# Expert gates of two latent tiles scattered to memory by an adding indirect DMA, and two norm barriers removed

## The chip, the cores and the metric

One core of one Trainium2 chip runs the whole kernel. The metric is device microseconds (us) of that core for one execution, as the median of several runs.

## The reference, cut to what matters

Two trunk layers run over 640 tokens: 512 latent tokens and 128 context tokens, 1024 features, fp32. A layer is attention in four branches, gates, an output product, a second norm, and then a mixture of experts ("peer"), which is what the change is mostly about:

```python
q = (x @ wq).reshape(n, PEER_HEADS, 2, PEER_HALF)                   # 8 heads, two halves
s = jnp.einsum('nhpd,hpkd->nhpk', q, subkeys)                       # 128 sub-keys a half
sv, si = lax.top_k(s, PEER_TOPK)                                    # 16 of 128, twice
cand = sv[:, :, 0, :, None] + sv[:, :, 1, None, :]                  # 256 pairs
cv, ci = lax.top_k(cand, PEER_TOPK)                                 # 16 experts a head
experts = e1 * PEER_KEYS + e2                                       # of 16384
gates = jax.nn.softmax(cv, axis=-1)
u = jnp.take(u_tab, ec, axis=0); a = gelu(einsum('cd,ckd->ck', xc, u))
v = jnp.take(v_tab, ec, axis=0); out = einsum('ck,ckd->cd', gc * a, v)
```

Each token so picks 128 (expert, gate) pairs, 16 in each of 8 heads. Two heads of a token may pick the same expert; within one head all 16 differ.

## The kernel before, in words

The program is written by hand, engine by engine, with semaphores between them: the order in each engine's function is the order of execution. `phase_end` is a barrier of PE, ACT, DVE and POOL. SP issues the loads, ACT the stores.

**The expert stage.** For latent tokens nothing is gathered. All 16384 experts are computed in 128 chunks of 128 experts. A chunk's u block (512 KB) is loaded by SP, ACT casts its high part (`high_u`, L1029), DVE or POOL subtracts to get its low part (`low_u`, L1332 on DVE, L1505 on POOL), PE multiplies in three passes of 8 products (`u_chunk`, L763, 24 products of 128x512), ACT applies gelu (L1036) and stores the activations. Afterwards, in the v stage (L803), the activations are loaded again, multiplied on DVE by the gate of each (expert, token), L1458, and multiplied with the v blocks.

**The gates.** The v stage needs a table of gates by expert and token, which is nearly all zeros. For each tile of 128 tokens DVE first makes the choice (`choose`: maxima, indices, replacements, L1245 to L1405), PE turns it (L776), and then 32 batches of 4 tokens follow. In a batch DVE builds 8 one-hot tiles (L1433, L1434), PE multiplies them in 4 products (L785), ACT copies the result (L1090) and stores it later (L1046). PE does half a u chunk after each batch.

**The context tile** is treated by rows: its 128 u rows for each of 128 picks are gathered by POOL with an indirect DMA (`rows_of`, L1577) into a ring of four buffers, DVE takes the dot product of each (`dot`, L1413), POOL may fetch row set k once dot k-4 is done. DVE has one dot in each batch.

**Order of the stage.** The context tile is chosen first, then the latent tiles 0 to 3. PE does 12 chunks ahead (`AHEAD`), then for each latent tile 12 chunks beside the next choice and 16 chunks beside 32 batches (`BESIDE`), and 4 chunks at the end. The low parts of chunks that run beside a choice are made by POOL, those beside the batches by DVE. POOL also loads the next tile's sub-key scores (L1589) when a choice is done.

**The two norms.** After attention, barrier 2 ends, the heads of branch A are normed (ACT squares L987, PE sums L462, ACT root L990, DVE reciprocal and product L1304, L1306), barrier 3 follows, and the gate products (L473) begin. After the output product (`wout`, L462) comes barrier 4, then norm 2: ACT squares L826, PE sums, ACT root L828, DVE reciprocal L1145, barrier 5.

## Time and profile before

| | |
|---|---|
| median of 3 runs | 5435.64 us (5434.37 to 5435.89) |
| the profiled execution, its own time | 5430.56 us |
| its span in the trace | 5428.8 us |
| mean granted TensorE clock | 0.958 of full |
| PE busy | 5107.0 us, 94% of the span |
| DVE, ACT, POOL busy | 59%, 31%, 24% |

The page lists busy time by engine, the span in 40 slices, the DMA queues, and the chain of work that ended last: who released whom, backwards from the last instruction. "PEld" is PE's weight load, which overlaps its products. In a row `A <-B` means that an engine was idle and then released by B. Times of separate rows are of the profiled execution, counted from the start of its span. The second layer repeats the first 2648 us later.

### The profile page before, as it was taken

How to read it: one execution, taken by the hardware profiler on the slowest of the kernel's cores; microseconds unless marked ns; L12 is line 12 of the kernel's file. 1: busy time of each engine (PE TensorE's matmuls, PEld its weight loads, DVE VectorE, ACT ScalarE, POOL GpSimd, SP SyncE). 2: the span in 40 equal slices, each digit the busy share in tenths (PEclk: the TensorE clock that was granted, in tenths of full speed). 3: DMA queues.
4: the chain of work that ended last, by engine and by line, in shares of the span. 5: the costliest groups of instructions: out<-in, count | busy, mean ns of one | idle time of the engine just before them, and what ended most of it. 6: DMA issues, size and time to landing. Idle time of an engine off the chain costs nothing.

```text
span 5428.8 us, 68440 instructions
## 1 busy us (share of the span) xinstructions
PE 5107.0 (94%) x25520; PEld 4128.9 (76%) x25520; DVE 3206.4 (59%) x7233; ACT 1676.3 (31%) x2614; POOL 1322.4 (24%) x862
## 2 busy tenths in 40 slices
PE   4979899899999999999989798998899999999999
PEld 1846688677888887888867467977788888788887
DVE  1556411107998985666655753111488998766666
ACT  2324422222333332222232343212233333322222
POOL 1310022214344331111122001213244344211111
PEclk6978999999999999999999799999999999999999
DMA  6200022264877879888831000221367877888886
GB/s 227 71 30 1 11 72 69 71 256 161 273 247 258 277 255 313 291 292 288 288 104 54 15 1 30 72 65 63 129 215 261 280 261 241 314 287 291 292 288 222
DMA packets 349128, 981.98 MB, mean 181 GB/s; under 512 B 31648, under 2 KB 100128, under 8 KB 345504
## 3 DMA queue, kind: packets, MB, share of 16 engines
q1 hardware_dynamic: 215232, 553.19, 31.4%
q0 software_dynamic: 74880, 276.86, 14.5%
q10 hardware_dynamic: 58720, 148.04, 6.9%
q8 instruction: 179, 2.93, 0.2%
q14 instruction: 117, 0.96, 0.1%
HBM read 829.43 MB, written 148.54 MB: 180 GB/s over the span
## 4 chain that ended last, share of the span: by engine, by line
PE 85%; DVE 6%; DMA 3%; ACT 2%; POOL 1%; issue 1%; DVEq 1%; ACTq 0%; POOLq 0%; SPq 0%
PE PS L803 26%; PE PS L763 23%; PE PS L473 15%; PE PS L462 5%; PE PS L785 4%; PE PS L594 3%; PE PS L620 2%; PE PS L463 1%; DVE AR L1172 1%; PE PS L604 1%; POOL HR L1505 1%; DMA WR<-in_ada 1%; PE PS L564 1%; PE PS L751 1%; DVE SM L1211 1%
## 5 line engine op out<-in xcount | busy, mean ns | idle before, releaser
L803 PE MATMUL PS<-HB,VR 128*128 128x512 f32 x6144 | 1397.0, 390 | 17.2 <-DVE HB L1462 17.2
L803 PEld LDWEIGHTS PS<-HB,VR 128*128 128x128 f32 x6144 | 1156.2, 188 | 258.1 <-issue 18.1
L763 PE MATMUL PS<-HR,UR 128*128 128x512 f32 x4128 | 1013.3, 399 | 0.0
L1505 POOL TENSOR_TENSOR UR<-WR,UR 128x1024 fp32r<-128x1024 f32 x212 | 528.4, 2493 | 1784.2 <-ACT UR L981 933.9
L473 PE MATMUL PS<-HR,UR 128*128 128x320 f32 (+1 forms) x5952 | 924.5, 314 | 40.6 <-POOL HR L1505 40.0
L473 PEld LDWEIGHTS PS<-HR,UR 128*128 128x128 f32 x5952 | 887.6, 190 | 68.0 <-issue 45.4
L763 PEld LDWEIGHTS PS<-HR,UR 128*128 128x128 f32 x4128 | 768.2, 190 | 167.1
L1449 DVE TENSOR_TENSOR VR<-HT,VR 128x1024 fp32r<-128x1024 f32 x256 | 313.8, 1226 | 459.7 <-ACT VR L1102 398.0
L1102 ACT CAST VR<-HT 128x1024 fp32r<-128x1024 f32 x256 | 268.8, 1050 | 962.0 <-PE PS L803 959.5
L763 PE MATMUL PS<-HR 128*128 128x512 f32 x2016 | 486.8, 394 | 0.0
L763 PEld LDWEIGHTS PS<-HR 128*128 128x128 f32 x2016 | 372.2, 188 | 73.6
L1036 ACT ACTIVATE AR<-PS 128x512 f32<-128x512 f32 x256 | 153.3, 599 | 770.5 <-PE PS L763 753.9
L1434 DVE TENSOR_SCALAR AR<-CN,AR 128x128 f32<-128x128 f32 x1024 | 353.8, 346 | 0.0
L1433 DVE TENSOR_SCALAR AR<-CN,AR 128x128 f32<-128x128 f32 x1024 | 306.6, 300 | 28.6 <-issue 22.3
L1172 DVE RECIPROCAL AR<-AR 128x640 f32<-128x640 f32 (+2 forms) x40 | 172.5, 4312 | 190.0 <-ACT AR L882 189.8
L785 PEld LDWEIGHTS PS<-AR 128*128 128x128 f32 x2048 | 267.3, 191 | 22.6 <-DVE AR L1434 2.2
L1577 POOL DMA_INDIRECT HX<-in_vtab,AR x128 | 120.4, 940 | 627.7 <-DVE HX L1473 574.7
L785 PE MATMUL PS<-AR 128*128 128x128 f32 x2048 | 269.9, 275 | 0.0
L1090 ACT COPY AR<-PS 128x512 f32<-128x512 f32 x256 | 150.7, 589 | 325.1 <-PE PS L785 299.5
L1316 DVE TENSOR_TENSOR AR<-AR,PS 128x640 f32<-128x640 f32 x48 | 39.5, 823 | 348.1 <-PE PS L463 348.1
L1577 POOL DMA_INDIRECT AR<-in_urows,AR x128 | 163.2, 1275 | 269.7 <-DVE AR L1413 268.5
L594 PE MATMUL PS<-AR 32*128 32x512 f32 (+4 forms) x720 | 218.4, 486 | 10.8 <-ACT AR L896 10.8
(183 smaller groups left out, 5982.2 us busy)
## 6 DMA issues: line engine op xcount, KB each, us to landing
WR<-in_uT SPq DMA_DIRECT2D x256, 512.0 KB
HT<-in_vtab SPq DMA_DIRECT2D x256, 512.0 KB, 4.0
activations<-AR ACTq DMA_DIRECT2D x256, 256.0 KB
gates_by_expert<-AR ACTq DMA_DIRECT2D x128, 512.0 KB, 3.5
HW<-activations SPq DMA_DIRECT2D x256, 256.0 KB
WR<-gates_by_expert SPq DMA_DIRECT2D x64, 1024.0 KB
WR<-in_wgate SPq DMA_DIRECT2D x64, 640.0 KB, 3.9
WR<-in_ada SPq DMA_DIRECT2D x24, 1024.0 KB, 4.9
```

The lines of the kernel that those rows point to most:

```text
L462: pe.matmul(out(0, 512), lhsT, rhs(0, 512), start=start, stop=stop)
L473: last = pe.matmul(out(lo, hi), part(w, c), whole(h, c, lo, hi), start=start and i == 0, stop=stop and i == 2)
L594: last = pe.matmul(PF[:, at:at + hi - lo], q, k[:, lo:hi], start=True, stop=True)
L763: last = pe.matmul(bank(n % 2), u_part(n, w)[:, c, :], HR[:, h, c, 0:LAT], start=c == 0 and i == 0, stop=c == DC - 1 and i == 2)
L785: last = pe.matmul(bank(2 + m % 2)[:, P * k:P * k + P], HOT[:, m % 2, 2 * k, :], HOT[:, m % 2, 2 * k + 1, :], start=True, stop=True)
L803: last = pe.matmul(bank(d), VR[:, m % 4, w, P * d:P * d + P], HB[:, (m + 1) % 3, h, :], start=m == 0 and i == 0, stop=m == E1 - 1 and i == 2)
L1102: nc.scalar.copy(VR[:, m % 4, 0, :], VRAW[:, m % 4, :]).then_inc(vh_ready, 1)
L1433: nc.vector.tensor_scalar(HOT[:, m % 2, 2 * k, :], iota, EWT[:, 1, tok], None, ALU.is_equal)
L1434: last = nc.vector.tensor_scalar(HOT[:, m % 2, 2 * k + 1, :], iota, EWT[:, 0, tok], EWT[:, 2, tok], ALU.is_equal, ALU.mult)
L1449: nc.vector.tensor_tensor(VR[:, m % 4, 1, :], VRAW[:, m % 4, :], VR[:, m % 4, 0, :].bitcast(F32), ALU.subtract).then_inc(v_split, 1)
L1505: nc.gpsimd.tensor_tensor(dst, src, high.bitcast(F32), ALU.subtract).then_inc(sem_, 1)
L1577: pool.indirect_dma_start(dst, None, table, bass.IndirectOffsetOnAxis(ap=IDX.bitcast(U32)[:, k:k + 1], axis=0)).then_inc(sem_, 16)
```

## The change

**Scatter.** The gates of latent tiles 0 and 1 (`SCAT = 2`) no longer go through one-hot tiles. A table `gates_by_row` in memory (128 chunks x 128 experts x 256 tokens, 16.8 MB) is set to zero during attention by 8 stores of SP from a buffer that POOL clears. For these tiles DVE computes a row number for each pick, and POOL issues, for each of the 128 picks of a token tile, one indirect DMA that adds 128 single numbers (one for each token) into the table. After each head's 16 DMAs POOL waits until they have landed, since two heads may add to the same number. Tiles 2 and 3 keep the one-hot way, now with a whole chunk of PE in each batch instead of half a chunk. The v stage loads half of the gates from each table.

**Order.** The choices now come in the order tile 0, context, tile 1, tile 2, tile 3. PE does 36 chunks beside the first three choices, then for tiles 2 and 3 12 chunks and 32 chunks with 32 batches each, and 4 chunks. POOL makes no low parts in this stage: DVE makes all, twelve of them within and right behind each choice. SP loads the next tile's scores, not POOL. Each batch has two dots, not one. POOL's row fetches now stand between the scatters of tile 1, eight after each head.

**Norms.** The branch A norm has no barrier behind it: PE waits for it (`sub_done`) only ahead of the first product that reads the normed heads. Norm 2 has no barrier ahead of it: ACT squares each block of features as it is finished, and PE sums it in the loop of the output product, two blocks behind.

```diff
-AHEAD, BESIDE = 12, 16
+AHEAD, BESIDE = 12, 32
...
+SCAT = 2
+WIDE = SCAT * P
...
+                sp.wait_ge(zeroed, l + 1)
+                clear = gate_rows.rearrange("(n p t) a -> n p (t a)", p=P, t=4 * D)
+                for n in range(E1 * WIDE // (4 * D)):
+                    sp.dma_start(clear[n], UR[:, :, :, :].rearrange("p a b d -> p (a b d)").bitcast(F32)).then_inc(z_out, 16)
...
                 for n in range(E1):
                     load_u(n)
+                    if n - AHEAD - 3 in BEGIN[:-1]:
+                        i = BEGIN.index(n - AHEAD - 3)
+                        sp.wait_ge(picked, l * TILES + i + 1)
+                        sp.dma_start(S1, sub_rows[ORDER[i + 1]]).then_inc(ss_next, 16)
...
                 for j in range(2):
                     pe.wait_ge(sub_sq, l * 2 + (j + 1))
-                    both(cols(1024 * j), grp64, lambda lo, hi: HSQ[:, j, lo:hi], True, True).then_inc(sub_ss, 1)
-                phase_end(pe, l, 3)
+                    both(cols(2048 + 1024 * j), grp64, lambda lo, hi: HSQ[:, j, lo:hi], True, True).then_inc(sub_ss, 1)
...
                         last.then_inc(g_ready, 1)
+                        if k == 0:
+                            pe.wait_ge(sub_done, 2 * (l + 1))
...
-                phase_end(pe, l, 4)
-                norm(l, 1)
-                phase_end(pe, l, 5)
+                    if n >= 2:
+                        square_sums(l, n - 2)
+                for c in range(DC - 2, DC):
+                    square_sums(l, c)
+                phase_end(pe, l, 3)
...
-                for n in range(AHEAD):
+                for n in range(AHEAD * (SCAT + 1)):
                     u_chunk(n)
...
-                        u_chunk(n0 + AHEAD + m // 2, DC // 2 * (m % 2), DC // 2 * (m % 2 + 1))
+                        u_chunk(n0 + AHEAD + m)
...
+                    low_u(n0 + 2)
                     indices8(sub_keys, range(SUB // 2))
+                    low_u(n0 + 3)
                     indices8(sub_keys, range(SUB // 2, SUB))
...
-                        dot(g)
-                        if m % 2 == 0 and m >= 2:
-                            low_u(n0 + 13 + m // 2)
+                        if m >= 2:
+                            low_u(n0 + AHEAD + m)
+                        dot(2 * g)
+                        dot(2 * g + 1)
...
+                def scatter(t, h):
+
+                    for k in range(TOPK * h, TOPK * (h + 1)):
+                        pool.indirect_dma_start(gate_rows, bass.IndirectOffsetOnAxis(ap=SIDX.bitcast(U32)[:, t, k:k + 1], axis=0),
+                                                SW[:, t, k:k + 1], None, compute_op=ALU.add).then_inc(sc_out, 16)
+
+                def head_added(t, h):
+                    pool.wait_ge(sc_out, 16 * TOPK * (PH * (l * SCAT + t) + h + 1))
+
+                pool.wait_ge(z_out, 16 * (l + 1) * (E1 * WIDE // (4 * D)))
+                pool.wait_ge(picked, l * TILES + 1)
+                for h in range(PH):
+                    scatter(0, h)
+                    head_added(0, h)
+                pool.wait_ge(picked, l * TILES + 3)
+                for h in range(PH):
+                    scatter(1, h)
+                    for k in range(8 * h, 8 * h + 8):
+                        gather_u(k)
+                    head_added(1, h)
+                pool.nop().then_inc(scattered, 1)
+                for k in range(8 * PH, PICKS):
+                    gather_u(k)
```

POOL at the start of the expert stage, before (HR, UR: the low parts; S1 in HT: the scores; the rest: fetched rows of u):

```order
L1505 TENSOR_TENSOR UR<-WR,UR 128x1024 x2
L1589 DMA HT<-sub_key_scores 128x2048
L1577 DMA AR<-in_urows,AR 128x1024 x2
L1577 DMA HT<-in_urows,AR 128x1024
L1577 DMA WR<-in_urows,AR 128x1024
L1505 TENSOR_TENSOR HR<-WR,HR 128x8x128
```

And now, from the first instruction of the stage up to the second head of tile 1:

```order
L336 TENSOR_TENSOR IDLE<-CN 128x1
L1640 DMA gates_by_row<-AR 4194304x1 x144
L1629 DMA AR<-in_urows,AR 128x1024 x2
L1629 DMA HT<-in_urows,AR 128x1024
L1629 DMA WR<-in_urows,AR 128x1024
L1629 DMA AR<-in_urows,AR 128x1024 x2
L1629 DMA HT<-in_urows,AR 128x1024
L1629 DMA WR<-in_urows,AR 128x1024
L1640 DMA gates_by_row<-AR 4194304x1 x16
```

The first 144 scatters are the 128 of tile 0 and the first head of tile 1. The row fetches, which followed the context choice, now stand behind all of them and in eights between the heads.

DVE within the last third of a choice, before (L1383 to L1405 are the softmax's difference, the pair numbers and the weights):

```order
L1261 MAX_INDEX AR<-AR,HT 128x8 x8
L1383 TENSOR_TENSOR AR<-AR 128x128
L1392 TENSOR_TENSOR HT<-AR,CN 128x2048
L1395 TENSOR_TENSOR HT<-HT,AR 128x2048
L1397 TENSOR_REDUCE AR<-HT 128x128
L1401 TENSOR_REDUCE AR<-AR 128x8
```

And now, with the low parts of the u chunks (L1354) between:

```order
L1283 MAX_INDEX AR<-AR,HT 128x8 x8
L1354 TENSOR_TENSOR UR<-WR,UR 128x1024
L1413 TENSOR_TENSOR AR<-AR 128x128
L1422 TENSOR_TENSOR HT<-AR,CN 128x2048
L1425 TENSOR_TENSOR HT<-HT,AR 128x2048
L1427 TENSOR_REDUCE AR<-HT 128x128
L1354 TENSOR_TENSOR HR<-WR,HR 128x8x128
L1432 TENSOR_REDUCE AR<-AR 128x8
```

Ten low parts stand inside each choice and two right behind it; before, none did.

## Rows read from the trace of the kernel before

**Rows 1.** The page: the chain that ended last, share of the span by line.
```profile
PE PS L803 26%; PE PS L763 23%; PE PS L473 15%; PE PS L462 5%; PE PS L785 4%; PE PS L594 3%; PE PS L620 2%; PE PS L463 1%; DVE AR L1172 1%; PE PS L604 1%; POOL HR L1505 1%; DMA WR<-in_ada 1%; PE PS L564 1%; PE PS L751 1%; DVE SM L1211 1%
```
**Rows 2.** Chain pieces of layer 0's expert stage: start us, us, what.
```profile
1232.66 58.16 PE PS L763 x240
1484.90 63.65 PE PS L763 x276
```
**Rows 3.** Chain around the last batches of that stage.
```profile
2032.46 0.89 PE PS L785 x8
2033.35 2.79 PE PS L763 x12
```
**Rows 4.** PE's timeline: the last u products of layer 0.
```profile
2055.58 6.44 PE L763 MATMUL PS<-HR,UR 128*128 128x512 f32 x27
```
**Rows 5.** DVE's timeline: one choice of a latent tile, cut.
```profile
1483.08 0.29 DVE L1245 MAX8 AR<-HT 128x8 f32<-128x128 f32 x1
...
1524.02 4.34 DVE L1395 TENSOR_TENSOR HT<-HT,AR 128x2048 f32<-128x2048 f32 x1
...
1533.16 2.29 DVE L1395 TENSOR_TENSOR HT<-HT,AR 128x2048 f32<-128x2048 f32 x1
1535.53 2.29 DVE L1397 TENSOR_REDUCE AR<-HT 128x128 f32<-128x2048 f32 x1
```
**Rows 6.** DVE's timeline in a batch: dot, low part, then one-hots until the next dot.
```profile
1560.12 1.21 DVE L1413 SCALAR_TENSOR_TENSOR HT<-HT,PS 128x1024 f32<-128x1024 f32 x1
...
1561.26 1.22 DVE L1332 TENSOR_TENSOR UR<-WR,UR 128x1024 fp32r<-128x1024 f32 x1
1562.40 0.28 DVE L1433 TENSOR_SCALAR AR<-CN,AR 128x128 f32<-128x128 f32 x1
...
1564.21 1.22 DVE L1413 SCALAR_TENSOR_TENSOR WR<-WR,PS 128x1024 f32<-128x1024 f32 x1
```
**Rows 7.** Timeline of POOL and DVE: scores load, four row fetches in a row, next choice.
```profile
1300.38 0.75 POOL L1589 DMA_DIRECT2D HT<-sub_key_scores  x1
1301.43 1.01 POOL L1577 DMA_INDIRECT AR<-in_urows,AR  x1 [0.30 <-issue]
...
1305.24 0.94 POOL L1577 DMA_INDIRECT WR<-in_urows,AR  x1 [0.30 <-issue]
...
1307.05 0.29 DVE L1245 MAX8 AR<-HT 128x8 f32<-128x128 f32 x1 [11.30 <-issue]
```
**Rows 8.** POOL's timeline: a row fetch issued beside the one-hot tiles of a batch.
```profile
1575.71 1.68 POOL L1577 DMA_INDIRECT HT<-in_urows,AR  x1 [1.77 <-DVE HT L1413]
```
**Rows 9.** DMA issues: count, KB each, median us to landing.
```profile
out_st_kr<-AR ACTq DMA_DIRECT2D x2, 16.0 KB, 3.2
...
WR<-in_vtab,AR POOLq DMA_INDIRECT x64, 4.9
```
**Rows 10.** Timeline of layer 0's branch A norm, with the products ahead and behind.
```profile
640.48 0.57 PE L463 MATMUL PS<-AR,CN 128*128 128x128 f32 x2
...
649.09 0.88 DVE L1306 SCALAR_TENSOR_TENSOR HT<-HT,SM,AR 128x640 f32<-128x640 f32 x1
...
650.51 9.09 PE L473 MATMUL PS<-HR,UR 128*128 128x320 f32 x48
```
**Rows 11.** Timeline around norm 2 of layer 0: last residual, first and last sum, barrier.
```profile
1018.30 1.01 DVE L1322 SCALAR_TENSOR_TENSOR XT<-PS,MD,XT 128x512 f32<-128x512 f32 x2 [7.64 <-PE PS L463]
...
1020.27 1.12 PE L462 MATMUL PS<-AR,CN 128*128 128x512 f32 x2 [0.48 <-ACT AR L826]
...
1028.80 0.38 PE L463 MATMUL PS<-AR,CN 128*128 128x128 f32 x2
...
1034.40 0.06 DVE L332 MEMSET IDLE<- 128x1 f32 x1 [0.20 <-DVEq L342]
```
**Rows 12.** Busy time by stretch: attention and v stage of layer 0 (clock, DMA share, GB/s last).
```profile
369.00:638.00 269.00, 243.14 (x1315) 166.25 (x1314) 157.53 (x468) 132.47 (x349) 5.03 (x4) 0.90 0.02 6
2075.00:2760.00 685.00, 685.00 (x3023) 567.38 (x3022) 455.50 (x503) 195.14 (x249) 115.67 (x123) 1.00 0.84 283
```

More of the change, by code:

```diff
@@ L96 @@
 C_EPS = C_I16 + 16
-C_ALL = C_EPS + 1
+C_ROW = C_EPS + 1
+C_ALL = C_ROW + 1
 TRIG = 6 * LAT
@@ L234, in build @@
         n_ = Arena(AR, 0, AF)
+        n_.take(12 * TOK)
         NSQ, NSTD, NRS = n_.take(DC, TOK), n_.take(TOK), n_.take(TOK)
@@ L319, in build @@
         a_in, g_in = [sem(f"activations_in{k}") for k in range(4)], [sem(f"gates_in{k}") for k in range(2)]
+        zeroed, z_out, sc_out, scattered = sem("zeros_made"), sem("gate_rows_cleared"), sem("gate_rows_out"), sem("gate_rows_done")
+        gs_in = [sem(f"gate_rows_in{k}") for k in range(2)]
         hw_ready, hbh_ready, h_ready, v_used = (sem(n) for n in ("expert_gated", "expert_gated_high", "expert_gated_split", "v_used"))
@@ L499, in norm, with square_sums @@
                 last.then_inc(ss_ready, 1)
+            def square_sums(l, c):
+                pe.wait_ge(sq_ready, l * (2 * DC) + (DC + c + 1))
+                last = both(cols(2048), ones, lambda lo, hi: NSQ[:, c, lo:hi], c == 0, c == DC - 1)
+                if c == DC - 1:
+                    last.then_inc(ss_ready, 1)
             def project(l, n):
@@ L766, in u_chunk @@
                         last.then_inc(u_used, 1)
-                for n in range(AHEAD):
+                for n in range(AHEAD * (SCAT + 1)):
                     u_chunk(n)
-                for t in range(LTILES):
-                    n0 = AHEAD + PER_TILE * t
+                for t in range(SPREAD):
+                    n0 = BEGIN[SCAT + 1 + t]
                     for n in range(n0, n0 + AHEAD - 1):
                         u_chunk(n)
-                    pe.wait_ge(picked, l * TILES + t + 2)
+                    pe.wait_ge(picked, l * TILES + SCAT + t + 2)
                     for i in range(3):
@@ L1003, in _ @@
                     sigmoid(l, DC - 1, k)
-                for n in range(2):
-                    high(l, B_WQ + n)
-                phase_end(act, l, 4)
                 norm(l, 1)
-                phase_end(act, l, 5)
+                high(l, B_WQ + 1)
+                phase_end(act, l, 3)
                 high_h(l, 1)
@@ L1414, in dot, with expert_number @@
                                                    accum_out=DOT[:, k:k + 1]).then_inc(dotted, 1)
-                choose(0, EWC)
-                nc.vector.scalar_tensor_tensor(EWC[:, 0, :], EWC[:, 0, :], float(PK), EWC[:, 1, :], ALU.mult, ALU.add)
-                dve.drain()
-                nc.vector.tensor_scalar(IDX.bitcast(U32), EWC[:, 0, :], GN[:, G_FIRST:G_FIRST + 1], None, ALU.add)
-                dve.drain().then_inc(picked, 1)
-                for t in range(LTILES):
-                    n0 = AHEAD + PER_TILE * t
-                    choose(t + 1, EW)
+                def expert_number():
+                    nc.vector.scalar_tensor_tensor(EW[:, 0, :], EW[:, 0, :], float(PK), EW[:, 1, :], ALU.mult, ALU.add)
+                    dve.drain()
+                for i in range(SCAT + 1):
+                    choose(i, BEGIN[i])
+                    expert_number()
+                    if ORDER[i] == LTILES:
+                        nc.vector.tensor_copy(WC, EW[:, 2, :])
+                        nc.vector.tensor_scalar(IDX.bitcast(U32), EW[:, 0, :], GN[:, G_FIRST:G_FIRST + 1], None, ALU.add)
+                    else:
+                        t = ORDER[i]
+                        nc.vector.tensor_copy(SW[:, t, :], EW[:, 2, :])
+                        nc.vector.tensor_scalar(EW[:, 1, :], EW[:, 0, :], float(WIDE), CN[:, C_ROW:C_ROW + 1], ALU.mult, ALU.add)
+                        dve.drain()
+                        nc.vector.tensor_scalar(SIDX[:, t, :].bitcast(U32), EW[:, 1, :], float(P * t), None, ALU.add)
+                    dve.drain().then_inc(picked, 1)
+                    low_u(BEGIN[i] + AHEAD)
+                    low_u(BEGIN[i] + AHEAD + 1)
+                for t in range(SPREAD):
+                    n0 = BEGIN[SCAT + 1 + t]
+                    choose(SCAT + 1 + t, n0)
                     dve.nop().then_inc(picked, 1)
-                    dve.wait_ge(ewt_ready, l * LTILES + t + 1)
+                    low_u(n0 + 12)
+                    dve.wait_ge(ewt_ready, l * SPREAD + t + 1)
                     settled(dve)
+                    low_u(n0 + 13)
                     for m in range(BATCHES):
```

175 lines of the change are left out of this document (90 added, 85 removed).

## The prediction

> **What bounds the kernel now.** I read the chain of waits first [rows 1]: almost all of it is PE, the v stage (L803, 26%), the u products (L763, 23%) and the gate products (L473, 15%). The one-hot products that the change halves (L785) are 4% of it. So PE sets the end, and one-hot work is worth what it takes on PE, not what it takes on DVE. The edits lie in the expert stage before the v stage, which begins in layer 0 at 1232.66 [rows 2] and whose last product ends at 2055.58 + 6.44 = 2062.0 [rows 4]: 829.4 us. Next I read PE's unit prices from the chain: 276 u products take 63.65 us [rows 2], so a chunk of 24 takes 5.54; half a chunk takes 2.79 and the 4 one-hot products of a batch 0.89 [rows 3]. 128 chunks and 128 batches make 709 + 114 = 823 us of 829: the stage is PE from end to end. DVE in a batch takes 1.81 us for the 8 one-hot tiles (1562.40 to 1564.21), 1.14 for a dot and 1.14 for a low part every second batch [rows 6], 3.5 us against PE's 3.68: nearly full, but not the bound.
>
> **One-hot batches removed.** 64 of 128 a layer at 0.89 us of PE: **-57 us a layer**. A remaining batch now has a whole chunk, PE 5.54 + 0.89 = 6.43 us; DVE needs 1.81 + 1.14 + two dots 2.28 = 5.2 us. DVE does not bound it.
>
> **Low parts moved to DVE.** Twelve stand in and behind each choice. A choice's own work runs from 1483.08 to 1535.53 + 2.29 = 1537.8, 54.7 us; one product in it took 4.34 us where its twin took 2.29 [rows 5], beside POOL's subtraction, which goes: 52.7. Ten low parts inside add 11.4 and the tail (sum, weights, row numbers, some eight small instructions) an estimated 2.3: 66.4 us to "picked". Then the next scores must be loaded. Before, that took from 1300.38 to 1307.05 [rows 7], 6.7 us; SP now does it without POOL in between, and the two low parts behind the choice lie beside it. Period 73.1 us against PE's 12 x 5.54 = 66.4. Three periods and the fourth choice end at 3 x 73.1 + 66 = 285 us, where PE alone would be at chunk 47 at 260 plus 3 us of its slow start (240 products in 58.16 us [rows 2]): **+22 us a layer**. The fifth choice has its scores early, and DVE enters it some 12 us ahead of PE: nothing.
>
> **POOL: the scatters.** No row shows an adding scatter. The nearest row is the row fetch, also an indirect DMA of 128 entries: 0.94 us busy, and 1.25 us from start to start when nothing blocks it (1301.43 to 1305.24, three intervals with their 0.30 of issue) [rows 7]. I take s = 1.25 us. Bounds: below, 0.75, the busy time of a direct DMA on POOL [rows 7]; above, 1.68 + 0.30 = 1.98, the fetch that falls beside DVE's one-hots [rows 8]. Small transfers land 3.2 us after issue [rows 9].
> Tile 0's scatters begin at 66 us (first choice) and take 8 x (16 x 1.25 + 3.2) = 186: until 252. Tile 1 was picked at 213 and starts then; its first head goes out until 272, and its first four fetches until 277, in time for the first batch at 290. But POOL's fetches number 4 to 7 wait for dots 0 to 3, so its second head starts only at 297. From here each of the 7 heads costs 16 x 1.25 = 20 us in which no row is fetched, and then a chain: the first row lands 4.9 us after issue [rows 9], two dots 2.3, the next batch's one-hots and low part 3.0, two dots 2.3, the eighth fetch 1.25, together 13.8. That is 33.8 us for four batches, where PE needs 4 x 6.43 = 25.7. DVE stands in a dot, its next one-hots stand behind it, and PE waits for them. 297 + 7 x 33.8 = 534, the last batches' dots and chunk 79 bring PE to 549; PE alone from 285 needs 5.5 + 0.7 + 32 x 6.43 = 212, so 497: **+52 us a layer**. Some two issues a head fall beside one-hots and take 0.74 longer [rows 8], 8 x 1.5 = **+12**. In the second one-hot tile POOL has only two fetches a batch, 2.5 to 4 us of 6.43: nothing.
> PE's idle pieces are some 8 us each. If it restarts at a lower clock, POOL still sets the period: I add nothing.
>
> A rule bears on the +12. The Trainium skill (GPSIMD Engine Reference, Key points) says that GpSimd shares its SBUF interfaces with VectorE, with contention against instructions in a two-port mode "or with two SBUF inputs". The traces agree for the one-hots (1.68 against 0.94 us). By its second half the low parts and dots would hold issues too, and if a third of the 256 scatters paid 0.74 the layer would have 63 us more, not 12; the fetches of the v stage that run beside two-input products at 0.94 us speak against it.
>
> **Zeroing.** 16.8 MB; at the 283 GB/s of the v stage it takes 59 us, in an attention stage of 269 us whose DMA share is 0.02 [rows 12]. POOL has 5 us of work there. Nothing; uncovered it would be 59 us a layer.
>
> **v stage.** The gate product becomes two of half size; DVE is busy 455 of 685 us there and PE all of it [rows 12]. The same bytes are loaded. Nothing.
>
> **Branch A norm.** Before, PE's sums end at 641.1 and the gate products start at 650.51 [rows 10]. Now 48 of them, about 9 us, run while DVE norms; the first product that reads the normed heads waits until 650.0. From there all is as before, minus these 9: **-9 us a layer**.
>
> **Norm 2.** Last residual 1018.30, barrier passed 1034.40 [rows 11]. The squares are hidden now, but PE's sums are not: the output product is PE-bound (DVE waits 7.64 us a block), so the 6 sums in its loop push its end by 6 x 1.1 = 6.7 us (8 took from 1020.27 to 1029.18). Then come the last residual 1.0, its square and sum, some 1.8, and the 5.2 from last sum to barrier (1029.18 to 1034.40), with a cast and the root's table load of ACT now between: 14.7 and 1 to 2 against 16.1. **0**, between -1.5 and +1.
>
> **Sum.** -57 + 22 + 52 + 12 - 9 = +20 us a layer, +40 in two: 5430.56 + 40 = 5470.6 for the profiled execution. The median of the runs stands 5.1 above that execution: **5476 us**, +0.7%. About 0.2% (11 us) is what a measurement of this kernel can tell from no change.
>
> **Rivals.**
> 1. *The scatters hide, and PE stays the bound: faster.* The point is s: POOL's period 16 s + 13.8 falls to PE's 25.7 at s = 0.75. Then the layer has -57 + 22 - 9 = -44: 5348 us. At s = 0.94 (busy time alone, the 0.30 of issue not paid) 16 s + 13.8 is 28.8 and the layer stands at about -25: 5386. The two signs meet near s = 1.1, only 0.15 below the row's spacing. For it: a scatter moves 512 bytes where a fetch moves 512 KB, and the fetches may land sooner than 4.9 us. Against it: POOL's issue time is of 128 entries, not of bytes.
> 2. *The adding scatter is dearer than a fetch: much slower.* To add, the old number must be read too, three accesses an entry where a fetch has two. Half again of 0.94 and 0.30 of issue makes s = 1.71. Tile 0 then ends at 66 + 8 x 30.6 = 311, the first head of tile 1 and its fetches at 352, seven periods of 41.2 bring 640, PE is at chunk 80 at 655: POOL costs 158, the layer +114 (no separate port term is large beside it, 0 to 12 left in), 5664 us. At the upper bound 1.98 the same steps give 724, the layer +183: 5802. The Trainium skill (Collectives: The Full Stack, Why ReduceScatter is half of AllGather) says that an add needs two source reads, two read descriptors per chunk on one ring; by it the fetch is too low a price for the scatter. No row here shows that.
> 3. *The parts cancel*: s near 1.1, within 11 us of before.
> That the batches would not go, or a barrier not, is excluded by the order of instructions.
>
> **Chances.** The forecast (s 1.15 to 1.4: 5445 to 5520) 0.34; rival 2 with all above 1.4, 0.25; rival 1, 0.32; rival 3, 0.09. So slower 0.59, faster 0.32, same 0.09. Signs are mixed, so the range runs from s = 0.75 to s = 1.98: 5345 to 5810.
>
> **What would show it.** Right: POOL's scatters start 1.25 us apart; tile 0's last lands near 250 us of the stage; in the first one-hot tile PE stops once for each head for about 8 us, released by one-hots (DVE) that stood behind a dot that waited for a row fetch; that tile takes some 265 us from its first batch to chunk 80, the next 206; the gate products start 9 us earlier after attention; norm 2 as before. Wrong if POOL is idle between heads, if PE is whole in that tile, if the spacing is far from 1.25, or if low parts make PE wait in the batches too. A stage of about 790 us would be rival 1, one over 900 rival 2.

## The result, and the profile after

The changed kernel takes 6219.8 us (median of 4 runs), the kernel before 5435.0: 1.144 times as long, 95% interval 1.142 to 1.146. The forecast was 5476 us, slower by 0.7%, with a range to 5810: the sign was right, the size was not, and the time lies outside the range. The profiled execution took 6220.68 us with a span of 6218.8 (before 5430.56 and 5428.8), at a mean granted clock of 0.894 in place of 0.958. Among the runs of the experiments three executions, two of the kernel before and one of tile0_only, were in a slower state; the ratios leave them out, and without it tile0_only's median of 5665.3 would be 5660.8.

The page of the changed kernel: the clock in 40 slices, the software DMA queue, the chain that ended last by line (rows 1 before), and two groups of instructions (busy, mean ns of one, idle time ahead of them and what ended it).

```profile
PEclk6979999999577799999999799999965768999999
...
q0 software_dynamic: 147456, 268.76, 16.1%
...
PE PS L823 22%; POOL gates_by_row L1640 13%; PE PS L484 13%; PE PS L783 8%; PE PS L473 5%; PE PS L611 3%; PE PS L637 2%; DMA AR<-in_urows,AR 1%; DVE AR L1194 1%; PE PS L621 1%; PE PS L474 1%; PE PS L805 1%; POOL HR L1558 1%; DMA gates_by_row<-AR 1%; DMA WR<-in_ada 1%
...
L1640 POOL DMA_INDIRECT gates_by_row<-AR x512 | 856.5, 1673 | 741.6 <-issue 564.1
...
L805 PE MATMUL PS<-AR 128*128 128x128 f32 x1024 | 151.0, 295 | 833.3 <-DVE AR L1482 833.3
```

Before, the chain had no scatters and POOL was 1% of it. Now the scatters (L1640) are 13% and the u products (L783) have shrunk from 23% to 8%. PE waited 833 us in two layers ahead of its one-hot products (L805). An issue is busy 1.67 us on the mean, and POOL was idle for 564 us ahead of scatters although nothing that the profile knows was to be waited for ("issue"). The two low stretches of the clock, 5 to 7 tenths, are those waits of PE.

A measure that serves below is the **stage**: layer 0's expert stage, from the matmul behind the barrier (L338) to the first v product. It is 838.6 us before (1232.08 to 2070.7) and 1240.8 now (1233.71 to 2474.5). That is 402 us a layer more, all of the difference of 790 and a little over. A **quiet** head is one that is scattered while DVE makes no choice. The first and the second **one-hot tile** are the token tiles 2 and 3, which keep the one-hot way, with the u chunks beside them.

POOL's timeline in the changed kernel, where tile 0's scatters begin: start us, us, and in brackets the idle time ahead of each and what ended it.

```profile
1303.78 2.04 POOL L1640 DMA_INDIRECT gates_by_row<-AR  x1 [69.85 <-DVEq L1464]
1306.12 1.57 POOL L1640 DMA_INDIRECT gates_by_row<-AR  x1 [0.30 <-issue]
1308.00 1.56 POOL L1640 DMA_INDIRECT gates_by_row<-AR  x1 [0.30 <-issue]
1312.86 1.58 POOL L1640 DMA_INDIRECT gates_by_row<-AR  x1 [3.30 <-issue]
1314.74 1.57 POOL L1640 DMA_INDIRECT gates_by_row<-AR  x1 [0.30 <-issue]
1316.62 1.56 POOL L1640 DMA_INDIRECT gates_by_row<-AR  x1 [0.30 <-issue]
1320.28 1.56 POOL L1640 DMA_INDIRECT gates_by_row<-AR  x1 [2.10 <-issue]
```

Two things are to be seen. An adding scatter of 128 entries keeps POOL busy for 1.56 us where a fetch of 128 rows took 0.94 [rows 7]. And the first three go out some 2 us apart, then POOL stands for 3.3 us; from there on one to three go out between pauses of 1.8 to 5.7 us. The eight heads of tile 0 run from 1303.78 to 1681.3, 47 us a head where 23 had been forecast; the last three, with no choice beside them, take 41.

Busy time by stretch in layer 0 (columns: length, then PE, PEld, DVE, ACT and POOL, each with its number of instructions, then granted clock, DMA share, GB/s):

```profile
1530.00:1727.00 197.00, 2.73 (x12) 1.89 (x10) 0.28 (x1) 1.53 (x2) 118.53 (x78) 0.52 0.19 5
1727.00:2148.00 421.00, 199.52 (x905) 165.84 (x905) 153.58 (x377) 57.44 (x84) 241.81 (x171) 0.73 0.51 136
2148.00:2447.00 299.00, 295.39 (x1408) 245.51 (x1407) 250.38 (x670) 92.30 (x132) 64.41 (x68) 0.99 0.82 277
```

For 197 us PE does nothing: it has done the first batch of the first one-hot tile and wants the one-hots of the second batch, DVE stands in the first dot ahead of them, the row for that dot has not been fetched, and the fetch stands in POOL's queue behind tile 0's scatters and the first head of tile 1. In the next 421 us PE is busy less than half the time: seven more times it stops for 29.4 to 32.5 us, 30.9 on the mean. Then, with all scatters gone, it is full. POOL's timeline shows the period of a head, from the first fetch behind one head's scatters to the first fetch behind the next, and PE's shows one of the stops:

```profile
1722.25 1.00 POOL L1629 DMA_INDIRECT AR<-in_urows,AR  x1 [0.31 <-issue]
...
1736.18 2.67 POOL L1640 DMA_INDIRECT gates_by_row<-AR  x1 [0.30 <-issue]
...
1780.39 1.00 POOL L1629 DMA_INDIRECT AR<-in_urows,AR  x1 [0.30 <-issue]
```

```profile
1790.29 2.08 PE L805 MATMUL PS<-AR 128*128 128x128 f32 x8 [29.36 <-DVE AR L1482]
```

Eight fetches with the dots that they wait for take 13.9 us (1722.25 to 1736.18), then 16 scatters 44.2: 58 us, and 59.1 on the mean of seven, where PE needs 25.7.

### The profile page after: what moved, and what is told of

The parts are those of the page before. It is cut to its first block, busy times and chain, and to the rows that moved or that the text cites. A ratio compares the mean times of both kernels' runs of the same rounds, so it can differ in the third digit from the quotient of the medians.

```text
span 6218.8 us, 65850 instructions
## 1 busy us (share of the span) xinstructions
PE 5046.3 (81%) x24476; PEld 4051.8 (65%) x24476; DVE 3098.5 (50%) x6595; ACT 1603.1 (26%) x2478; POOL 1776.6 (29%) x1244
## 3 DMA queue, kind: packets, MB, share of 16 engines
q0 software_dynamic: 147456, 268.76, 16.1%
## 4 chain that ended last, share of the span: by engine, by line
PE 59%; POOL 15%; issue 10%; DVE 7%; DMA 4%; ACT 2%; DVEq 1%; ACTq 0%; POOLq 0%; SPq 0%
PE PS L823 22%; POOL gates_by_row L1640 13%; PE PS L484 13%; PE PS L783 8%; PE PS L473 5%; PE PS L611 3%; PE PS L637 2%; DMA AR<-in_urows,AR 1%; DVE AR L1194 1%; PE PS L621 1%; PE PS L474 1%; PE PS L805 1%; POOL HR L1558 1%; DMA gates_by_row<-AR 1%; DMA WR<-in_ada 1%
## 5 line engine op out<-in xcount | busy, mean ns | idle before, releaser
L1640 POOL DMA_INDIRECT gates_by_row<-AR x512 | 856.5, 1673 | 741.6 <-issue 564.1
L783 PE MATMUL PS<-HR,UR 128*128 128x512 f32 x4128 | 1017.3, 404 | 14.3 <-DVE UR L1354 14.3
L484 PEld LDWEIGHTS PS<-HR,UR 128*128 128x128 f32 x5952 | 887.1, 190 | 65.5 <-issue 45.5
L783 PEld LDWEIGHTS PS<-HR,UR 128*128 128x128 f32 x4128 | 790.8, 194 | 198.2 <-DVE UR L1354 18.6
L805 PE MATMUL PS<-AR 128*128 128x128 f32 x1024 | 151.0, 295 | 833.3 <-DVE AR L1482 833.3
L1558 POOL TENSOR_TENSOR UR<-WR,UR 128x1024 fp32r<-128x1024 f32 x132 | 314.8, 2386 | 1590.2 <-ACT UR L1005 945.5
L805 PEld LDWEIGHTS PS<-AR 128*128 128x128 f32 x1024 | 145.6, 208 | 849.7 <-DVE AR L1482 840.2
L1444 DVE SCALAR_TENSOR_TENSOR AR<-AR,PS 128x1024 f32<-128x1024 f32 x128 | 152.0, 1214 | 940.8 <-DMA AR<-in_urows,AR 940.8
L783 PE MATMUL PS<-HR 128*128 128x512 f32 x2016 | 493.0, 401 | 12.0 <-DVE HR L1354 12.0
L783 PEld LDWEIGHTS PS<-HR 128*128 128x128 f32 x2016 | 386.8, 194 | 95.5 <-DVE HR L1354 14.2
L1113 ACT COPY AR<-PS 128x512 f32<-128x512 f32 x128 | 75.2, 588 | 844.1 <-PE PS L805 842.0
L1354 DVE TENSOR_TENSOR UR<-WR,UR 128x1024 fp32r<-128x1024 f32 x172 | 209.1, 1220 | 166.4 <-ACT UR L1051 161.9
L1629 POOL DMA_INDIRECT AR<-in_urows,AR x128 | 121.9, 952 | 331.4 <-DVE AR L1444 319.5
```

What stands on the lines that cost most here:

```text
L484: last = pe.matmul(out(lo, hi), part(w, c), whole(h, c, lo, hi), start=start and i == 0, stop=stop and i == 2)
L783: last = pe.matmul(bank(n % 2), u_part(n, w)[:, c, :], HR[:, h, c, 0:LAT], start=c == 0 and i == 0, stop=c == DC - 1 and i == 2)
L805: last = pe.matmul(bank(2 + m % 2)[:, P * k:P * k + P], HOT[:, m % 2, 2 * k, :], HOT[:, m % 2, 2 * k + 1, :], start=True, stop=True)
L1558: nc.gpsimd.tensor_tensor(dst, src, high.bitcast(F32), ALU.subtract).then_inc(sem_, 1)
L1629: pool.indirect_dma_start(dst, None, table, bass.IndirectOffsetOnAxis(ap=IDX.bitcast(U32)[:, k:k + 1], axis=0)).then_inc(sem_, 16)
L1640: pool.indirect_dma_start(gate_rows, bass.IndirectOffsetOnAxis(ap=SIDX.bitcast(U32)[:, t, k:k + 1], axis=0), SW[:, t, k:k + 1], None, comp ...
```

## The experiments

Twelve kernels. Stages are of layer 0; each time is a median, each ratio against runs of the kernel before on the same chip.

| run | time, us | ratio (95%) | stage, us |
|---|---|---|---|
| no_scatter | 5339.9 | 0.9825 (0.9811 to 0.9839) | 802.5 |
| norms_only | 5409.7 | 0.9962 (0.9949 to 0.9975) | 837.8 |
| one_tile2k | 5411.1 | 0.9957 (0.9941 to 0.9973) | 842.2 |
| one_tile | 5461.9 | 1.0049 (1.0031 to 1.0068) | 864.0 |
| spread2k_plain | 5468.3 | 1.0055 (1.0034 to 1.0076) | 870.8 |
| spread2k | 5477.3 | 1.0078 (1.0063 to 1.0093) | 866.5 |
| plain2k | 5586.7 | 1.0282 (1.0261 to 1.0303) | 928.7 |
| plain_scatter | 5647.1 | 1.0394 (1.0379 to 1.0409) | 943.0 |
| tile0_only | 5665.3 | 1.0416 (1.0394 to 1.0437) | 963.4 |
| spread | 5703.9 | 1.0491 (1.0468 to 1.0513) | 983.4 |
| space2k | 5929.2 | 1.0915 (1.0899 to 1.0931) | 1100.3 |
| moved_only | 6213.9 | 1.1428 (1.1405 to 1.1452) | 1243.7 |

**No scatters at all.** This asks whether the other terms of the forecast hold.

```diff
-                for h in range(PH):
-                    scatter(0, h)
-                    head_added(0, h)
...
-                    scatter(1, h)
...
-                    head_added(1, h)
```

> The changed kernel without any scatter and without the waits for them (the gates of two latent tiles stay zero, so their expert sums are left out); zeroing, loads, choices and the low parts on DVE stay. If the scatters are the whole loss, the prediction's other terms are left: 64 batches fewer -57, low parts on DVE +22, norm -9 us a layer, stage near 829 - 57 + 22 = 794 us and 5430.6 - 88 = 5343 us for the profiled execution, PE whole in both one-hot tiles but for the start of the first. If DVE with all low parts is itself a bound (the rival), the first one-hot tile still shows PE waiting for one-hots in every batch, the stage is 830 us or more and the time no less than 5420 us.

Measured: 5339.9 us; the stage is 802.5 in layer 0 and 804.2 in layer 1, against 838.6 and 838.2 before. So everything in the change but the scatters gains 1.75%, and the scatters cost 438 us a layer. PE and its clock by stretch, then the start of the first one-hot tile:

```profile
1522.00:1728.00 206.00, 206.00 (x1025) 172.99 (x1024) 168.85 (x423) 65.32 (x96) 59.34 (x64) 1.00 0.91 307
...
1796.00:2002.00 206.00, 206.00 (x1022) 172.99 (x1021) 168.63 (x415) 64.57 (x95) 58.32 (x62) 1.00 0.89 297
```

```profile
1522.39 1.05 PE L805 MATMUL PS<-AR 128*128 128x128 f32 x8
1523.19 5.82 PE L783 MATMUL PS<-HR,UR 128*128 128x512 f32 x24
1528.86 1.05 PE L805 MATMUL PS<-AR 128*128 128x128 f32 x8
```

Both one-hot tiles take the 206 us of 32 x 6.43 with PE busy throughout, and a batch comes every 6.47 us. The rival that DVE with all low parts would bound the batches is out. The first batch is at 290.6 us of the stage; the forecast had 290.

**Tile 0's scatters alone.**

```diff
                 for h in range(PH):
-                    scatter(1, h)
                     for k in range(8 * h, 8 * h + 8):
                         gather_u(k)
-                    head_added(1, h)
```

> The changed kernel with tile 0's scatters alone (tile 1's are left out, its gates stay zero). It parts the 438 us a layer that the scatters cost: tile 0's heads end at 446 us of the stage, and the first fetches stand behind them, where PE wants the first at 290. If that start is one of two causes, the stage is 802 + 446 + 5 - 290 = 963 us, 5340 + 2 x 161 = 5662 us, and the other 277 us a layer are tile 1's heads between the fetches. If tile 1's heads alone were the loss (tile 0's hidden, as the prediction had it), 5345 us.

Measured: 5665.3 us, stage 963.4, both as expected. PE's waits have one entry of one-hots, twice (once a layer):

```profile
PE PS L805 <- DVE AR L1482: 318.6, 2, 159.7
```

So of the 438 us, 161 are the late first fetch, and 277 are tile 1's heads: one head of 41 before the first fetch, and seven periods of 59.1 (the seven from 1722.25 to 2135.96) against PE's 25.7, which is 41 + 7 x 33.4 = 275.

**More memory for descriptors, and its control.**

```diff
-                   dynamic_dma_scratch_size=1024)
+                   dynamic_dma_scratch_size=2048)
...
-        PT = t_.take(2, 640)
+        PT = QA
...
-        WC, IDX, DOT = p_.take(PICKS), p_.take(PICKS), p_.take(PICKS)
+        WC = GN[:, G_LAM:G_LAM + PICKS]
+        IDX, DOT = p_.take(PICKS), p_.take(PICKS)
```

> The changed kernel with twice the memory for the descriptors of POOL's indirect DMAs (2048 bytes a partition in place of 1024); two small buffers move for it (the turned probabilities into QA, the context weights into GN). Theory A (space): in the changed kernel the scatters go out 1.87 us apart in twos and threes and then pause 2 to 5 us, since three adding scatters fill the memory and the next waits until one has been worked off. Then here some seven go out in a row before the first pause, and if the DMA engines keep up the spacing is 1.87 us throughout: a head of tile 0 takes 16 x 1.87 + 3.0 = 33 us in place of 41, the expert stage near 990 us in place of 1212, 5780 us in all. Theory B (work-off rate): the 16 DMA engines work off one adding scatter in about 2.6 us whatever the memory; then the first six or seven go out in a row, but the head still takes some 40 us and the time stays within 1% of 6220 us. Theory C (the pauses have nothing to do with memory, they are in POOL's own routine): pattern and time as in the changed kernel.

> The control for the run with 2048 bytes: the changed kernel with the two small buffers moved, the descriptor memory left at 1024 bytes. If the memory is what let seven scatters go in a row in place of three, this one shows threes again and 6220 us within 0.3%. If the moved buffers did it, some 5930 us.

Measured: 5929.2 us with 2048 bytes; 6213.9 with the buffers moved alone (the line with 1024 kept), the same as the changed kernel. POOL's timeline with 2048 bytes, first, seventh and eighth scatter:

```profile
1295.07 2.05 POOL L1641 DMA_INDIRECT gates_by_row<-AR  x1 [69.89 <-DVEq L1465]
...
1306.76 1.56 POOL L1641 DMA_INDIRECT gates_by_row<-AR  x1 [0.30 <-issue]
1310.21 1.56 POOL L1641 DMA_INDIRECT gates_by_row<-AR  x1 [1.90 <-issue]
```

Seven go out in a row in place of three. In the control the fourth again waits 3.23 us. So it is the memory, theory A; C is out. The quiet heads of tile 0 take 34.7 us (two of them from 1532.49 to 1601.89) in place of 41, close to 16 x 1.86 + 3 = 33, so B, a limit of the DMA engines' rate near 2.6 us a scatter, is out for them as well. My 5780 us were too low all the same: beside the choices a head still takes 37 to 43, and in tile 1's part a period is some 50 us in place of 59, the pauses being shorter but not gone ("issue" idle time ahead of scatters 291 us of two layers, after 564; both hold the 0.30 of each issue, at most 154).

**Scatters that overwrite, with either memory.**

```diff
-                                                SW[:, t, k:k + 1], None, compute_op=ALU.add).then_inc(sc_out, 16)
+                                                SW[:, t, k:k + 1], None).then_inc(sc_out, 16)
```

> The changed kernel with scatters that overwrite in place of adding (a token that picks one expert in two heads keeps only the last weight, so that part of the result is left out). Theory A (the add makes it dear, by the read of the old number, a third access for each entry): busy time of an issue falls from 1.56 to about the fetch's 0.94 us, three accesses become two, so that five or more fit before a pause; spacing 1.25 to 1.6 us, stage 830 to 900 us in place of 1212, 5430 to 5600 us in all. Theory B (4-byte writes to memory are dear in themselves): busy time falls, the pauses grow by as much, a head of tile 0 still takes 36 to 41 us and the time stays above 6000 us.

> Scatters that overwrite (as in plain_scatter, so part of the result is left out) with 2048 bytes for descriptors. With 1024 seven of them went out in a row before a pause; if a plain scatter takes half the room of an adding one and the room is all there is, fourteen go here, about one pause in a head of 16 is left, and a head of tile 0 takes 16 x 1.26 + 3 = 23 us beside quiet engines in place of 25 to 26: stage some 20 us shorter than plain_scatter's, 5590 to 5620 us against 5647. If the DMA engines' rate makes the pauses, they come back behind the first fourteen and the time stays above 5630 us.

Measured: 5647.1 and 5586.7 us. POOL's timeline with 1024 bytes: the first, seventh and eighth scatter,

```profile
1299.73 1.47 POOL L1640 DMA_INDIRECT gates_by_row<-AR  x1 [69.85 <-DVEq L1464]
...
1307.83 0.96 POOL L1640 DMA_INDIRECT gates_by_row<-AR  x1 [0.30 <-issue]
1310.78 0.96 POOL L1640 DMA_INDIRECT gates_by_row<-AR  x1 [1.99 <-issue]
```

and with 2048 bytes the first, the fourteenth and the fifteenth:

```profile
1293.00 1.48 POOL L1641 DMA_INDIRECT gates_by_row<-AR  x1 [69.95 <-DVEq L1465]
...
1310.96 0.96 POOL L1641 DMA_INDIRECT gates_by_row<-AR  x1 [0.30 <-issue]
1314.88 0.97 POOL L1641 DMA_INDIRECT gates_by_row<-AR  x1 [2.96 <-issue]
```

Before the first pause, three and seven go out with the add, seven and fourteen without: an adding scatter takes about twice the room of a plain one, and the room grows with the memory. Without the add an issue is busy 0.96 us, the fetch's price. The add is thus the larger part of the damage: 1240.8 - 943.0 = 298 of the 438 us. The pauses were not all that expectation A made of it: the plain scatters with 1024 bytes still cost 141 us a layer, above the 830 to 900 us of stage that I had written down, since "seven in a row" still means one or two pauses in a head, and a plain scatter beside the choices takes up to 3.03 us. With 2048 bytes the fourteen came as expected; the stage is 14 us shorter and not 20, and 5586.7 us lies 3 us below what was written down. The rule that the forecast cited as rival 2's (the Trainium skill, Collectives: The Full Stack, Why ReduceScatter is half of AllGather: an add has two source reads and so two read descriptors) agrees with both halves, the price of an issue and the room that it takes; the runs show the effects, not the descriptors.

**The same work in another order.** Six heads of tile 0 first, then two scatters behind each pair of fetches in place of 16 in a row:

```diff
+                done = scatters(0, 96)
+                pool.wait_ge(picked, l * TILES + 2)
+                for k in range(PICKS):
+                    if k == 2 * BATCHES + 4:
+                        done = scatters(done, 36)
+                    gather_u(k)
+                    if k >= 5 and k % 2:
+                        done = scatters(done, 2)
+                done = scatters(done, SCAT * PICKS)
```

> The changed kernel with the same 256 adding scatters a layer in another order on POOL: tile 0's first six heads alone, then the row fetches with two scatters behind each pair of them (and 36 at the place between the two one-hot tiles), in place of 16 scatters in a row; a head still waits for the one before. Theory (order): in the changed kernel 16 scatters in a row hold up the fetches that the dots, and so PE, wait for; spread, each batch has 2 x 1.25 us of fetches and 2 x 1.87 us of scatters, 6.2 us against PE's 6.43, and the landing waits lie beside fetches. Tile 0's six heads take about 48 us each, so the fetches start near 356 us of the stage where PE wants them by 290: 66 us late; stage near 802 + 66 = 868 to 900 us (802 is the stage without scatters), 5475 to 5540 us. Rival (POOL's sum of work, pauses included): if a scatter costs 2.6 us wherever it stands, 256 x 2.6 + 160 = 826 us of POOL from 66 us on: stage 900 to 950 us, 5540 to 5640 us.

> The same spread order with 2048 bytes a partition for the descriptors. Tile 0's heads took 37 to 42 us each beside the choices with this memory, so six of them end near 66 + 6 x 38 = 294 us, in time for PE's first batch. By the order theory the stage is then 802 + 5 to 30 us (the scatters that fall beside DVE's one-hots take 2.6 us in place of 1.56, some one in four), 5350 to 5410 us, faster than the kernel before. Rival (POOL's sum): at 2.1 us a scatter 256 x 2.1 + 160 + 66 = 764, also below 802; so if this run stays above 5435 us, neither is right and contention with DVE is the larger price.

> The same as the spread order with 2048 bytes, but the first head of each tile is scattered without adding, which is the same result, since a token's 16 picks of one head are 16 different experts and the memory is zero before. 32 of 256 scatters cost 0.96 in place of 1.56 us of POOL: 10 us of one head alone before the first fetch, if that start is late at all. Between 0 and 10 us a layer below the run before: 5340 to 5410 us.

Measured: 5703.9, 5477.3 and 5468.3 us. The order alone takes 257 us from the stage (1240.8 to 983.4) with every scatter kept; order and memory together 374, so that 64 us of the 438 are left. With 1024 bytes the time lies above both written ranges. The rival, POOL's sum of work wherever it stands, comes nearest: (892 busy + 468 of "issue" + 52 of landing) / 2 = 706 us of scatters a layer and 128 x 1.3 = 166 of fetches, from 70 on, make 942, and the stage is 983; the other 41 I have not traced. Of the 149 us that PE waits for one-hots in layer 0, 72.5 are one wait at the start of the first one-hot tile, which the order theory had put at 66. spread2k is 0.8% slower than the kernel before and not 0.5 to 1.5% faster. Its busy times in the first one-hot tile:

```profile
1520.00:1730.00 210.00, 191.39 (x928) 158.18 (x927) 155.76 (x377) 59.58 (x89) 165.41 (x121) 0.96 0.90 269
```

POOL issues 121 DMAs there, busy 165 us, and with 0.30 each for the next (36) that is 201 of 210: POOL is the bound. Its scatters average 1.72 us: in layer 0 the 146 that overlap an instruction of DVE with two inputs in SBUF (here the low parts and the softmax products of the choices) average 1.85, the other 110 1.57. The version with each tile's first head unadded (`compute_op=ALU.add if k >= TOPK else ALU.bypass`, the same result) is 9 us lower. That is inside the 0 to 10 us a layer that were expected below spread2k, but the two intervals overlap, and layer 0's stage is 4 us longer: no gain is shown.

**One tile scattered, three by one-hot products.** If two tiles are too much for POOL, is one right?

```diff
-AHEAD, BESIDE = 12, 32
+AHEAD, BESIDE = 12, 21
...
-SCAT = 2
+SCAT = 1
```

with u chunks cut to fit 21 beside 32 batches, dots spread over 96 batches, and one scatter behind each pair of fetches.

> Gates of one latent tile scattered, three by one-hot products (96 batches, 21 chunks beside 32 of them), spread order on POOL, 2048 bytes a partition for descriptors, both norms without barriers. By the prices measured so far: the stage without scatters was 802 us; 32 batches more at 0.89 are +28, one choice fewer with all its low parts in front of the one-hots about -7: 823 us, if POOL's 128 scatters (some 2.0 us each, 256 us) and 128 fetches (160 us) hide in the 750 us that it has, where 256 scatters did not. That is 838 - 823 = 15 us a layer below the stage before and 10.7 for the norms: 5431 - 2 x 25.7 = 5379 us, ratio 0.990. Rival (DVE: a batch has 1.81 us of one-hots, 1.33 dots and 0.66 low parts at 1.14, 4.1 us against PE's 4.53, and issues beside them take longer): PE waits a little in every batch and the stage is 835 us or more, 5405 us, no better than the norms alone.

> The same with 1024 bytes for descriptors as in the changed kernel. If the spread order leaves POOL room for the pauses (128 x 2.7 + 160 = 506 us of 750), the time is that of the run before within 0.2%; only the first three heads before the first fetch are slower (48 in place of 38 us each, and one head fewer stands there). If pauses reach the fetches (a fetch that finds no memory for its descriptors waits too), 10 to 40 us a layer more: 5400 to 5460 us.

Measured: 5411.1 us with 2048 bytes, 5461.9 with 1024. The first beats the kernel before by 0.4%, as much as the norms alone, so the scattering itself gains nothing: the stage is 842.2 (839.6 in layer 1) and not 823. The batches run near PE's rate (PE busy 148.2, 141.2 and 146.4 us of three stretches of 150). PE waits for one-hots once, for 5.5 us, so the rival of a wait in every batch is out; the rest of the missing 19 us is spread over the stage in pieces that I have not traced. With 1024 bytes the stage is 22 us longer, and PE waits 30.9 us for one-hots: the pauses do reach the fetches, at the upper end of what was expected for that case.

**Only the norms' edits**, on the kernel before (barriers 3 and 4 out, sums of squares into the output product, as in the change).

```diff
-                phase_end(pe, l, 3)
...
+                        if k == 0:
+                            pe.wait_ge(sub_done, 2 * (l + 1))
...
-                phase_end(pe, l, 4)
-                norm(l, 1)
-                phase_end(pe, l, 5)
+                    if n >= 2:
+                        square_sums(l, n - 2)
```

> The kernel before with only the two norms' edits (both barriers out). By the prediction's terms: branch A norm -9 us a layer, norm 2 between -1.5 and +1, so 5435 - 18 = 5417 us, between 5414 and 5419. By what the profile of the changed kernel shows (the gate products start early, but then wait for the second normed head): -5 us a layer, 5425 us. Rival: what the first norm gives, ACT and DVE lose again in the gate loop, and the time is within 0.1% of before.

Measured: 5409.7 us, 0.9962 (0.9949 to 0.9975). The forecast's price for it was 5417, inside the interval; the -5 us that I read from the changed kernel's profile was too little. With one_tile2k (0.9957), from which it can't be told, it is the fastest kernel of this study that computes everything, and far simpler.

## Why the prediction was right or wrong

**What failed: the price of a scatter, s = 1.25 us with an upper bound of 1.98.** The bound was built from rows of fetches: the dearest fetch and its issue time. The changed kernel shows 1.56 + 0.30 = 1.86 for a scatter that nothing disturbs, which lies inside the bounds. What no row had was the pause when the memory for descriptors is full, and the forecast named no such resource. With it a quiet head takes 41.1 us, so that s is (41.1 - 3.0) / 16 = 2.4, and 2.9 beside the choices, where a head takes 51; between the fetches it is 44.2 / 16 = 2.8. An estimate by the forecast's own steps with s = 1.86, the busy time and issue gap without any pause, gives some 5740 us: the dearer instruction explains some 260 of the 744 us that the forecast missed, and the pauses, with what the scatters lose beside DVE, the rest. Put into the forecast's own steps, the measured sizes give the measured time: tile 0 ends at 70 + 8 x 47 = 446 us of the stage in place of 252, which makes PE wait 160 us; tile 1's first head 41; seven periods of 59.1 in place of 33.8 against PE's 25.7. The sum is 160 + 41 + 234 = 435, and 438 were measured. The forecast's POOL term was 52 + 12 = 64.

**The path was right.** PE does stop once a head in the first one-hot tile, released by one-hots that stood behind a dot that waited for a fetch behind scatters; the stops are 31 us and not 8. The stop of 199 us ahead of them had not been forecast: tile 0's scatters were to end in time. The second one-hot tile is whole. The chain of 13.8 us between two heads measured 13.9 and, one head later, 15.1.

**One-hot batches removed, -57, low parts on DVE, +22.** Together -35 for the stage; the run without scatters shows -36.1 and -34.0. The second choice began 74.75 us behind the first (forecast 73.1).

**POOL's port, +12.** The mean of 512 scatters is 1.67 against 1.56 undisturbed, 58 us of POOL in two layers, 29 a layer. The size was low, and the forecast had the wrong partner in it: the one-hots. While DVE stood still (1531 to 1727) the longest of 74 issues took 1.57 us. Of layer 0's 256 scatters, 72 overlap an instruction of DVE with two inputs in SBUF (low parts, sums and products of the choice). The 47 that begin while such an instruction runs average 2.20 us; the 25 that have begun before it average 1.57. Of the 30 that run beside other work of DVE alone, one-hots and dots among it (a dot reads one of its inputs from PSUM), none takes more than 1.59. The longest took 3.10:

```profile
1406.27 2.29 DVE L1399 TENSOR_TENSOR HT<-AR 128x2048 f32<-128x2048 f32 x1
```

```profile
1406.87 3.10 POOL L1640 DMA_INDIRECT gates_by_row<-AR  x1 [1.76 <-DMA gates_by_row<-AR]
```

The kernel before already shows it. The fetch of [rows 8], which the forecast took to be slowed by one-hots, falls into a low part:

```profile
1575.37 1.21 DVE L1332 TENSOR_TENSOR HR<-WR,HR 128x1024 fp32r<-128x1024 f32 x1
```

```profile
1575.71 1.68 POOL L1577 DMA_INDIRECT HT<-in_urows,AR  x1 [1.77 <-DVE HT L1413]
```

In that stage, 63 fetches beside one-hots alone average 0.98 us and none takes more than 1.08, while the 55 that begin within 0.4 us behind the start of a low part average 1.68. The forecast's argument against the low parts was misread too: of the 123 fetches of layer 0's v stage that the trace has, not one runs beside an instruction of DVE, so their 0.94 us says nothing of two-input products. The Trainium skill (GPSIMD Engine Reference, Key points) names just that, contention against instructions with two SBUF inputs, and the trace agrees; the forecast had cited it and priced the one-hots.

**Zeroing, nothing.** Eight stores a layer drain in the first 46 us of attention. Attention of layer 0 was 269.4 us in the changed kernel and 261.3 before, but in layer 1 261.8 and 266.3, and part of the extra time has a granted clock of 0.84 between 500 and 550 (0.96 before), long after the stores. A small price is not excluded: in all twelve kernels of this study that zero a table layer 0's attention takes 262.5 to 276.4 us, and 261.3 and 261.5 in the two that don't.

**Branch A norm, -9.** Here is PE in the run without scatters:

```profile
638.43 0.59 PE L338 MATMUL PS<-CN 128*128 128x2 f32 x2 [6.08 <-POOLq L342]
...
643.58 7.56 PE L484 MATMUL PS<-HR,UR 128*128 128x320 f32 x48
652.85 1.12 PE L473 MATMUL PS<-HT,WR 128*128 128x512 f32 x2 [1.71 <-DVE HT L1328]
...
655.04 7.28 PE L484 MATMUL PS<-HR,UR 128*128 128x320 f32 x48
```

From the barrier to the second set of gate products it takes 16.6 us; before it took 25.9 (635.62 to 661.51). That is -9.3. In layer 0 of the changed kernel it took 20.7, for a reason worth seeing, on DVE, POOL and PE:

```profile
654.63 2.88 DVE L1328 SCALAR_TENSOR_TENSOR HT<-HT,SM,AR 128x640 f32<-128x640 f32 x1
```

```profile
654.50 2.34 POOL L1558 TENSOR_TENSOR UR<-WR,UR 128x1024 fp32r<-128x1024 f32 x1 [13.08 <-ACT UR L1005]
```

```profile
657.57 2.07 PE L473 MATMUL PS<-HT,WR 128*128 128x512 f32 x2 [4.23 <-DVE HT L1328]
```

DVE's last product began 0.13 us behind the start of POOL's low part and took 2.88 us; a moment before, with POOL idle, it took 0.88. PE then waited 4.2 us in place of 1.7, and its next pair of products took 2.07 us in place of 1.12, at a granted clock of 0.60 between 655 and 660.

**Norm 2, between -1.5 and +1.** From the barrier behind attention to the barrier behind norm 2, in layer 1 (before, then without scatters):

```profile
3312.27 0.59 PE L338 MATMUL PS<-CN 128*128 128x2 f32 x2 [6.08 <-POOLq L342]
...
3710.75 0.59 PE L338 MATMUL PS<-CN 128*128 128x2 f32 x2 [5.16 <-DVEq L342]
```

```profile
3273.65 0.58 PE L338 MATMUL PS<-CN 128*128 128x2 f32 x2 [6.08 <-POOLq L342]
...
3661.60 0.58 PE L338 MATMUL PS<-CN 128*128 128x2 f32 x2 [5.94 <-DVEq L342]
```

398.5 and 387.95: both norms gain 10.5, so norm 2 gives -1.2. The forecast's terms other than POOL's therefore stand, and their sum without POOL, 5343 us for the profiled execution, met the run without scatters (5345.2).

**The chances.** Rival 2 (0.25) was right that an adding scatter is dearer than a fetch, and a stage over 900 us was its mark; but it stopped at its upper bound of 5802, and the time lay 418 us beyond. That the added read is the reason was argued from a page and is not shown. The range was built from bounds on an instruction, and what decided most was how many of them the descriptor memory holds.

## What to carry to other kernels

Before many small indirect DMAs are put on POOL, look for more than the time of one issue: send a burst of them and see in the profile after how many the idle time marked "issue" starts; here an add about halved that number, and doubling the descriptor memory doubled it. Put what PE's chain needs (the fetches) ahead of bulk issues in the same queue and spread the bulk thinly behind; the same work in another order was worth 257 us of a stage of 1241. And price a change in parts that can be taken alone: here the two norms' edits by themselves gave 0.4%, and the one-hot products that the scatters were to replace gave nothing that a version with scatters could keep.

## What was not expected of the hardware

- An adding indirect DMA of 128 entries of 4 bytes keeps POOL busy for 1.56 us, a plain one for 0.96, a fetch of 128 rows of 4 KB for 0.94.
- POOL stands with no wait in the profile when the descriptor memory is full: the first pause comes after 3 adding or 7 plain scatters with 1024 bytes a partition, after 7 or 14 with 2048. Software-queue packets grew by 144 for each adding scatter and by 32 for each plain one (147,456 and 90,112 against 73,728 without scatters, over 512).
- POOL's issues grow beside DVE's instructions with two inputs in SBUF and not beside its other work: from 1.56 to 2.20 us on the mean of the 47 that begin while one runs, to 3.10 at most, against at most 1.59 beside one-hots and dots. A scatter that begins before the DVE instruction keeps its 1.57. The other way round, a DVE product with two such inputs grew from 0.88 to 2.88 us beside a low part of POOL that had begun first.
- In the 197 us in which PE stood still the granted clock was 0.52, near the lower of its two levels (1.2 GHz of 2.4); over the stretch with a wait in every head it was 0.73, and back at 0.99 once PE was full. In those periods it cost nothing further, since POOL set the pace.
